# First attention: the sum of squares as two passes over rounded numbers, and the rotation's partner rows projected by extra weight columns

## The reference

```python
kv = (rmsnorm(ckv, ckv_g) @ w_ukv).reshape(B, L, 12, 64 + 64)
k = concatenate([kv[..., :64], broadcast(k_rope, 12 heads, 32)], axis=-1)   # 96 per head
k = rmsnorm(k, k_g)
q = (rmsnorm(h[..., :256], cq_g) @ w_uq).reshape(B, L, 12, 96)
q = rmsnorm(q, q_g)                       # x * rsqrt(mean(x * x) + EPS) * g
# rotation of the last 32 of the 96, on latent tokens:
x1, x2 = x[..., :16], x[..., 16:]
x = concatenate([x1 * cos - x2 * sin, x1 * sin + x2 * cos], axis=-1)
p = softmax(q @ k.T * 96 ** -0.5) ; o = p @ v
```

## Time and profile before

| | |
|---|---|
| median of 3 runs | 3061.49 us (3056.06 to 3071.42) |
| the profiled execution's own time | 3064.81 us, its span 3063.0 us |
| TensorE busy | 2933.3 us, 96% of the span |
| VectorE busy | 1799.2 us, 59% |
| ScalarE busy | 1360.8 us, 44% |
| GpSimd busy | 701.9 us, 23% |

### The profile page before, as it was taken

The page is one execution under the profiler, slowest core; times in us unless marked ns, Lnnn a source line. Parts: engine busy times, 40 slices in busy tenths (PEclk is TensorE's granted clock), DMA queues, the critical chain, the costliest instruction groups (busy, mean ns, idle before and its releaser), DMA issues. The chain is left out here.

```text
span 3063.0 us, 38159 instructions
## 1 busy us (share of the span) xinstructions
PE 2933.3 (96%) x14042; PEld 2109.6 (69%) x14042; DVE 1799.2 (59%) x2476; ACT 1360.8 (44%) x2162; POOL 701.9 (23%) x509
## 2 busy tenths in 40 slices
PE   5998999999999999999999999979999999999999
PEld 2563444444478888889998887844448788888887
DVE  5124656455535877789863444356643887777442
ACT  3014665656633544445653432136662544445231
POOL 0001555455520133330000000034550133331000
PEclk8998999999999999999999999989999999999999
DMA  9920000000020222224664431122211122224453
GB/s 372 369 98 2 4 3 3 4 2 2 7 110 35 77 83 83 83 83 159 210 196 125 145 102 49 41 66 66 64 45 49 63 78 85 84 85 146 137 171 100
DMA packets 101718, 282.14 MB, mean 92 GB/s; under 512 B 12129, under 2 KB 27745, under 8 KB 94562
## 3 DMA queue, kind: packets, MB, share of 16 engines
q1 hardware_dynamic: 101570, 280.16, 27.4%
HBM read 237.25 MB, written 27.26 MB: 86 GB/s over the span
## 5 line engine op out<-in xcount | busy, mean ns | idle before, releaser
L1367 ACT ACTIVATE z_wh<-part 128x512 fp32r<-128x512 f32 x266 | 166.5, 629 | 335.3 <-PE PS L1238 211.4
L1743 DVE TENSOR_TENSOR z_wdl<-part,z_wdh 128x512 fp32r<-128x512 f32 (+3 forms) x208 | 148.7, 721 | 255.5 <-ACT z_wdh L1420 255.2
L1236 PE MATMUL PS<-s_uh,z_wh 128*128 128x512 f32 x736 | 286.6, 389 | 0.0
L1238 PE MATMUL PS<-s_uh,z_wl 128*128 128x512 f32 x736 | 286.6, 389 | 0.0
L1237 PE MATMUL PS<-s_ul,z_wh 128*128 128x512 f32 x736 | 286.5, 389 | 0.0
L1420 ACT ACTIVATE z_wdh<-part 128x512 fp32r<-128x512 f32 (+3 forms) x208 | 135.2, 655 | 303.7 <-DMA part<-in_w_down 302.7
L1664 DVE TENSOR_TENSOR z_wl<-part,z_wh 128x512 fp32r<-128x512 f32 x266 | 218.2, 833 | 46.3 <-ACT z_wh L1367 46.3
L2400 POOL TENSOR_TENSOR X<-X 128x1024 f32<-128x1024 f32 x96 | 229.4, 2389 | 59.6 <-ACT X L2635 58.7
L1223 POOL TENSOR_TENSOR part<-part,part 128x512 f32<-128x512 f32 x38 | 56.8, 1495 | 777.1 <-DMA part<-in_w_up 777.1
L2635 ACT ACTIVATE X<-PS 128x512 f32<-128x512 f32 x252 | 145.9, 593 | 143.8 <-PE PS L2422 135.5
L2731 DVE TENSOR_REDUCE part<-PS 128x1 f32<-128x512 f32 (+1 forms) x312 | 161.9, 580 | 13.7 <-PE PS L2534 12.9
(11 more groups left out here) (412 smaller groups left out, 7594.6 us busy)
## 6 DMA issues: line engine op xcount, KB each, us to landing
part<-in_w_up SPq DMA_DIRECT2D x132, 512.0 KB, 3.3
part<-in_mod_w SPq DMA_DIRECT2D x48, 1024.0 KB, 7.2
part<-in_w_down SPq DMA_DIRECT2D x96, 256.0 KB, 2.7
gated<-part SPq DMA_DIRECT2D x44, 512.0 KB, 2.6
part<-gated SPq DMA_DIRECT2D x87, 256.0 KB, 5.5
part<-in_w_down SPq DMA_DIRECT2D x32, 384.0 KB, 3.1
part<-in_w_down SPq DMA_DIRECT2D x32, 320.0 KB, 3.2
part<-in_w_down SPq DMA_DIRECT2D x48, 192.0 KB, 2.4
```

Source lines behind the costliest of these rows:

```text
L1236: pe.matmul(bank_, w_h, x_h, start=start, stop=False, skip_group_check=further)
L1238: return pe.matmul(bank_, w_l, x_h, start=False, stop=stop, skip_group_check=further)
L1367: act.activation(wh[i][:, :], full[b][i], ACT.Copy).then_inc(s["hi"], 1)
L1743: dve.tensor_tensor(wdl[j][:, :width(e)], wd[j][:, :width(e)], wdh[j][:, :width(e)].bitcast(F32), ALU.subtract).then_inc(s["wdl"], 1)
```

## The change

It does two things in the preparation of each head.

*Sum of squares.* The square is rounded to fp32r by ScalarE (`skh` for keys, `sqh` for queries), VectorE subtracts the rounded number from the square (`square_low`, giving `skl` or `sql`), and `squares` makes two fp32r matmuls by rounded ones (`unity`) into the same bank, in place of one of plain float32. The shared rows 64 to 96 and the ones are rounded once ahead of the loop. `squares` now waits for the subtraction (`sql`) and no longer only for the Square.

*Rotation.* The projection weights of the queries have 128 columns for 96: 32 more hold the partner features in swapped order (`TURNED`). The matmul by `rot0` goes, as does the copy to `raw` of units 3 and 4. VectorE's `turn` has a second operation on 32 rows, partner times gain times signed sine to `raw[64:96]`, and `unit` adds those 32 rows to `t1` and multiplies by the reciprocal root. The sine table has the rows 96 to 128 for this.

```diff
-        WQ = [big(O_A + 8 * T + 20 * 64 + b * 256, 256) for b in range(2)]
+        WQ = [big(O_A + 8 * T + 20 * 64 + b * W_QK, W_QK) for b in range(2)]
...
                         elif w == 5:
                             pe.wait_ge(s["sq"], 6 * p + 5)
-                            pe.wait_ge(s["t1"], 2 * p + 2)
+                            pe.wait_ge(s["ts"], 2 * p + 2)
...
                             for k in range(2):
-                                mm = pe.matmul(ps(PB[w], hi - lo, slice(0, A_QK)), wq[b][:, 96 * k:96 * k + 96],
+                                mm = pe.matmul(ps(PB[w], hi - lo), wq[b][:, k * P:(k + 1) * P],
...
                     def squares(p, w):
-                        pe.wait_ge(s["sq"], 6 * p + w + 1)
-                        if w == 4:
-                            pe.wait_ge(s["out"], 6 * p + 4)
+                        pe.wait_ge(s["sql"], 6 * p + w + 1)
                         at_least(pe, "lo", 6 * p + w - 1)
-                        src = sk[0:A_QK, lo:hi] if w < 3 else sq[w % 2][0:A_QK, :hi - lo]
-                        pe.matmul(ps(NB[w % 2], hi - lo, slice(0, A_QK)), ones[0:A_QK, 0:A_QK], src,
-                                  start=True, stop=True).then_inc(s["nt"], 1)
-                        if 3 <= w < 5:
-                            if w == 3:
-                                pe.wait_ge(s["t1"], 2 * p + 1)
-                            pe.matmul(ps(TB, hi - lo, slice(0, A_QK)), rot0[:, 0, :],
-                                      raw[w % 2][0:A_QK, :hi - lo], start=True, stop=True).then_inc(s["rt"], 1)
+                        for x in (skh, skl) if w < 3 else (sqh[w % 2], sql[w % 2]):
+                            part = x[0:A_QK, lo:hi] if w < 3 else x[0:A_QK, :hi - lo]
+                            mm = pe.matmul(ps(NB[w % 2], hi - lo, slice(0, A_QK)), unity[0:A_QK, :], part,
+                                           start=x in (skh, sqh[w % 2]), stop=x in (skl, sql[w % 2]))
+                        mm.then_inc(s["nt"], 1)
...
                             act.activation(sk[0:64, lo:hi], ps(PB[w], n, slice(0, 64)), ACT.Square).then_inc(s["sq"], 1)
+                            act.wait_ge(s["sq"], 6 * p + w + 1)
+                            act.activation(skh[0:64, lo:hi], sk[0:64, lo:hi], ACT.Copy).then_inc(s["sqh"], 1)
...
                             act.activation(sq[w % 2][0:96, :n], ps(PB[w], n, slice(0, 96)), ACT.Square)\
                                 .then_inc(s["sq"], 1)
+                            act.wait_ge(s["sq"], 6 * p + w + 1)
+                            act.activation(sqh[w % 2][0:96, :n], sq[w % 2][0:96, :n], ACT.Copy).then_inc(s["sqh"], 1)
...
+                    act.activation(skh[64:96, :], sk[64:96, :], ACT.Copy).then_inc(s["kh0"], 1)
+                    act.activation(unity[:, :], ones[:, 0:A_QK], ACT.Copy).then_inc(s["kh0"], 1)
...
-                        dve.wait_ge(s["rt"], v + 1)
-                        T_ = ps(TB, n, slice(0, 96))
-                        dve.tensor_tensor(T_, T_, rope[0:96, 1, lo:hi], ALU.mult).then_inc(s["ts"], 1)
                         dve.wait_ge(s["ts"], v + 1)
-                        dve.tensor_tensor(t_, t_, T_, ALU.add).then_inc(s["ta"], 1)
+                        dve.tensor_tensor(t_[64:96], t_[64:96], raw[w % 2][64:96, :n], ALU.add).then_inc(s["ta"], 1)
...
+                        dve.scalar_tensor_tensor(out=raw[w % 2][64:96, :n], in0=ps(PB[w], n, slice(96, P)),
+                                                 scalar=sml[96:P, W_G0:W_G0 + 1], in1=rope[96:P, 1, lo:hi],
+                                                 op0=ALU.mult, op1=ALU.mult).then_inc(s["ts"], 1)
+
+                    def square_low(p, w):
+                        lo, hi = CH[w % 3]
+                        n = hi - lo
+                        dve.wait_ge(s["sqh"], 6 * p + w + 1)
+                        if w < 3:
+                            out_, in_, h_ = skl[0:64, lo:hi], sk[0:64, lo:hi], skh[0:64, lo:hi]
+                        else:
+                            out_, in_, h_ = [x[w % 2][0:96, :n] for x in (sql, sq, sqh)]
+                        dve.tensor_tensor(out_, in_, h_.bitcast(F32), ALU.subtract).then_inc(s["sql"], 1)
...
                         if kind == "prep" and 3 <= n < 5:
                             turn(p, n)
+                        if kind == "prep" and n < 6:
+                            square_low(p, n)
                         if kind == "prep" and 0 < n < 7:
                             unit(p, b, n - 1)
...
+                    dve.wait_ge(s["kh0"], 1)
+                    dve.tensor_tensor(skl[64:96, :], sk[64:96, :], skh[64:96, :].bitcast(F32), ALU.subtract).then_inc(s["kh0"], 1)
```

More of the change, by code:

```diff
@@ L40 @@
 A_SCALE = A_QK ** -0.5
+TURNED = [*range(A_QK), *range(80, 96), *range(64, 80)]
+W_QK = 2 * P + A_NOPE
 C_HEADS, C_KV, C_HD = 12, 4, 64
@@ L88, in rope @@
         return np.cos(a).T.astype(np.float32), np.sin(a).T.astype(np.float32)
-    rope0 = np.zeros((A_QK, 2, T), np.float32)
+    rope0 = np.zeros((P, 2, T), np.float32)
     rope0[:, 0] = 1
@@ L94, in constants @@
         rope0[b:b + 16, 0, :SEQ], rope0[b:b + 16, 1, :SEQ] = cs, sn
+    rope0[96:112, 1], rope0[112:128, 1] = -rope0[64:80, 1], rope0[80:96, 1]
     rope1 = np.zeros((P, 2, T), np.float32)
@@ L2074, in _ @@
                     sp.wait_ge(s["ab"], 7)
-                    sp.dma_start(ROPE[0:A_QK], a["rope0"]).then_inc(s["tab"], 16)
+                    sp.dma_start(ROPE[:, :, :], a["rope0"]).then_inc(s["tab"], 16)
                 @block.gpsimd
@@ L2267, in heads0 @@
             assert o == O_A + 8 * T + 20 * 64
-            o += 512
+            o += 2 * W_QK
             wq = WQ
@@ L2274, in heads0 @@
             rest += 2 * T
-            raw, sq = [[Xf[:, rest + (2 * x + n) * BANK:rest + (2 * x + n + 1) * BANK] for n in range(2)] for x in range(2)]
-            t1 = [take(BANK) for _ in range(2)]
+            raw, t1 = [[Xf[:, rest + (2 * x + n) * BANK:rest + (2 * x + n + 1) * BANK] for n in range(2)] for x in range(2)]
+            sql = [place(f"h0_sql{n}", o + n * BANK, BANK) for n in range(2)]
+            sq = [take(BANK) for _ in range(2)]
+            sqh = [place(f"h0_sqh{n}", 9088 + n * BANK, BANK) for n in range(2)]
             lnb = take(BANK)
@@ L2280, in heads0 @@
             osb = take(BANK + P)
+            skh, skl = place("h0_skh", O_MIX + 5 * T, T), place("h0_skl", -(-o // 32) * 32, T)
+            unity = place("h0_unity", 10 * A_HEADS * 64, A_QK)
             rope = ROPE
@@ L2302, in heads0 @@
                      ("one", "one1", "pad", "pad1", "S", "P", "PV", "raw", "rawc",
-                      "sq", "nt", "rt", "ln", "rinv", "t1", "ts", "ta", "out", "hi", "lo", "cast", "vs", "mx", "mc", "mn", "mrow",
+                      "sq", "sqh", "sql", "kh0", "nt", "ln", "rinv", "t1", "ts", "ta", "out", "hi", "lo", "cast", "vs", "mx", "mc", "mn", "mrow",
                       "mr", "o", "bc", "lnr", "rs", "fin", "ad")}
@@ L2488, in project @@
                         if w < 3:
-                            mm = pe.matmul(ps(PB[w], hi - lo, slice(0, 64)), wq[b][:, 192:256], H[:, 2, lo:hi],
+                            mm = pe.matmul(ps(PB[w], hi - lo, slice(0, 64)), wq[b][:, 2 * P:W_QK], H[:, 2, lo:hi],
                                            start=True, stop=True)
@@ L2524, in step @@
                             for c, (lo, hi) in enumerate(CH):
-                                if (n, c) == (0, 1):
-                                    pe.wait_ge(s["out"], 6 * p + 5)
                                 if (n, c) == (0, 2):
@@ L2585, in project @@
                             act.activation(sk[0:64, lo:hi], ps(PB[w], n, slice(0, 64)), ACT.Square).then_inc(s["sq"], 1)
+                            act.wait_ge(s["sq"], 6 * p + w + 1)
+                            act.activation(skh[0:64, lo:hi], sk[0:64, lo:hi], ACT.Copy).then_inc(s["sqh"], 1)
                         else:
                             at_least(act, "nt", 6 * p + w - 1)
-                            if w == 3:
-                                at_least(act, "out", 6 * p)
-                            act.activation(raw[w % 2][0:96, :n], ps(PB[w], n, slice(0, 96)), ACT.Copy)\
-                                .then_inc(s["rawc"], 1)
+                            if w == 5:
+                                act.wait_ge(s["ta"], 2 * p + 1)
+                                act.activation(raw[1][0:96, :n], ps(PB[w], n, slice(0, 96)), ACT.Copy)\
+                                    .then_inc(s["rawc"], 1)
                             act.activation(sq[w % 2][0:96, :n], ps(PB[w], n, slice(0, 96)), ACT.Square)\
                                 .then_inc(s["sq"], 1)
+                            act.wait_ge(s["sq"], 6 * p + w + 1)
+                            act.activation(sqh[w % 2][0:96, :n], sq[w % 2][0:96, :n], ACT.Copy).then_inc(s["sqh"], 1)
                     def inverse(p, w):
@@ L3615 @@
     put(W_CKVG, cols(f["mla_ckv_g"][0]))
-    put(W_G0, f["mla_q_g"].T)
```

(3 more changed lines are left out.)

## The result

| | before | changed |
|---|---|---|
| median in one comparison | 3061.96 us | 3102.27 us (3098.90 to 3103.00, 4 runs) |
| ratio | | 1.0128, 95% interval 1.0113 to 1.0144 |
| the profiled execution's own time | 3064.81 us | 3098.90 us, its span 3097.1 us |
| TensorE busy | 2933.3 us | 2903.2 us |
| VectorE busy | 1799.2 us | 1882.0 us |

The change makes the kernel 40 us slower, with TensorE busy 30 us less. The forecast was 34 us more.

What follows compares the result with a forecast made beforehand. The ScalarE and VectorE chain up to VectorE's reduces, not TensorE, was taken to bound the kernel: 11 x 2.55 + 6 = 34 us on 3061.5 gives 3095 us. Likeliest case 3084 to 3107 (0.61); 8 in 10 from 3070 to 3115.

Steps and rivals of the forecast that it cites:

- The chain: Preparation of a head: square, sum, Ln, Exp, normalise, round, remainder on ScalarE and VectorE decides when the reduces start, not TensorE.
- The walk: Step-by-step timing of one head's six units from 397.25 us: reduces at 425.48 for 422.93, 2.55 us more a head.
- TensorE's waits: In a head's preparation: 6.4 us after the change, where before has about 0.4.
- its savings: TensorE work saved: 2.0 us on sums of squares and 1.8 on rotations, 3.8 us a head, 42 us over eleven preparations.
- The width of the projection: Query projection with 32 more outputs: costed at nothing, upper bound 1.4 us.
- The blocked subtractions: Units 2 and 4: a VectorE subtraction with two SBUF inputs waits for GpSimd's add; recorded over 1.5 and over 1 us.
- The rival without blocks: Subtractions each take 0.69 us at once: +0.8 us a head, +15 in all, 3076 us; chance 0.16.
- the case of a longer chain: Adds block a third subtraction or 32-row sum, or waits lower TensorE's clock: + 25 us, 3120 us; chance 0.10.
- The sum: Whole kernel: 11 x 2.55 + 6 = 34 us more, carried to the median: 3095 us.
- The first preparation: Start of the attention, with nothing to hide it: first normalising at 266.1, end at 284.8 for 278.76, +6 us.
- The 11 heads: Preparations in the attention loop: each 2.55 us longer, 11 x 2.55.
- a row of few partitions: VectorE's two new 32-row products: about the 0.7 us that a 512 operation takes whatever its rows.

Runs made afterwards that it cites:

- Experiment 6: Changed kernel with the squares summed in one rounded pass, remainders left out: 3050.2 us against 3061.4 before, ratio 0.9961.
- experiment 4: Only the rotation's half of the change, sum of squares left as one plain float32 matmul: 3055.5 us against 3059.5 before, ratio 0.9979.
- 9: Experiment 6 with four overwritten plain float32 matmuls a head in TensorE's waits: 3048.8 us against 3062.1 before, ratio 0.9953.
- 8: Experiment 4 with three overwritten plain float32 matmuls a head ahead of the maxima: 3045.1 us against 3061.4 before, ratio 0.9946.
- experiment 1: Changed kernel with squares of keys and of units 4 and 5 left in PSUM: 3094.3 us against 3059.5 before, ratio 1.0107.
- 2: Changed kernel with GpSimd's adds in rounds 3 and 4 cut to 32 columns, first add a memset: 3091.7 us against 3059.5 before, ratio 1.0088.
- 5: Changed kernel with unit 1 normalised on VectorE ahead of the subtraction of unit 2: 3097.9 us against 3061.4 before, ratio 1.0120.
- experiment 3: Only the two-pass rounded sum of squares, rotation by the `rot0` matmul as before: 3117.2 us against 3059.5 before, ratio 1.0181.
- experiment 11: Changed kernel, squares in SBUF, with four overwritten matmuls a head in TensorE's waits: 3096.9 us against 3062.1 before, ratio 1.0116.
- 10: Kernel before the change with three overwritten matmuls a head ahead of the maxima, a control: 3063.4 us against 3062.1 before, ratio 1.0003.
- 7: Experiment 1 with four overwritten plain float32 matmuls a head in TensorE's waits: 3080.8 us against 3061.4 before, ratio 1.0070.

## Why the prediction was right, point by point

**The chain sets the time, not TensorE: shown.** The reduces moved by 2.7 us a head (forecast 2.55) while TensorE's busy time in that part fell by 2.7 where no low stretch lies in it. Experiment 6 takes another 2.9 us of TensorE's work away from the part of experiment 4 and leaves it as long, and with the waits filled (9 against 8) the time doesn't fall either. The halves of the change go the same way: rotation alone shortens the chain by 1.2 us, squares alone lengthen it by 4.1 to 5.6, of which some may be the clock's.

**The walk.** Set against the timeline of the head that starts at 409.05 (11.80 later than the walk's start), it has the sum of unit 0 at 414.5 (measured 414.45), the rounding of unit 1 at 421.96 (421.96), that of unit 3 at about 431.0 (431.11) and the reduces at 437.28 (437.47). TensorE's waits were put too long: 6.4 us a head, where the three entries for the new subtraction and the partner product come to 4.6. So were its savings, though nothing hung on them: a pair of rounded sums takes 0.54 us and not 0.46 (0.31 from the first to the second, then 0.23). The width of the projection was costed at nothing, which is right: two passes of 512 columns with 128 outputs take 1.71 us from start to start (509.82 to 511.53 in experiment 4), and with 96 outputs 1.72 (410.19 to 411.91 before).

**The blocked subtractions: shown.** 2.23 and 1.23 us where the walk has 2.2 and 1.5, each held until GpSimd's add is through. They fall to 0.42 and 0.69 when one operand is in PSUM (experiment 1) or when the add is short (2), and that of unit 2 also when VectorE comes to it later (5). The Trainium skill's page SBUF — State Buffer, section "Who interferes with whom", says the same: a VectorE instruction with two SBUF inputs and a GpSimd instruction that reads SBUF block one another in full, the later one waiting, and a tensor_tensor with only one input in SBUF doesn't contend. These runs agree on both counts: 2.2 against 0.42 us.

**The rival without blocks: its price was wrong.** It was put at 3076, by the walk alone. Experiments 1 and 2 are that case, and measure 3094 and 3092; only with the waits filled is it 3081. What was missing is the low clock in the second part of a head, where it is paid for. The prediction named a falling clock only within the case of a longer chain. It came in the second part where the chain was shorter than the changed kernel's (experiments 1, 2, 4, 5 and 6), in one of ten heads of the changed kernel, and in none of experiment 3, whose chain is longer still. In the changed kernel three of the heads of 51.3 have a low stretch in the first part, where TensorE waits anyway, and the other six have none: all nine are equally long, and experiment 11, with fills, has reduces and heads of the same length. So the forecast came out right without a word on the clock. In that it had luck: nothing in it said that the clock would cost the changed kernel 1.6 us in one head of ten, and the kernel of experiment 1 as much in every head.

**The sum: sizes off.** It was 34; the trace has 39.3. The first preparation cost 7.5, not 6. Its first normalising comes 13.04 us behind the start, where before has 6.96: 6.1 more, and the walk has 5.2. From there to the reduces it is 1.4 more, and the walk has 0.9:

```profile
264.53 0.69 DVE L2687 TENSOR_TENSOR PS<-X,PS 96x512 f32<-96x512 f32 x1 [2.00 <-ACT PS L2608]
...
283.77 12.96 DVE L2749 TENSOR_REDUCE part<-PS 128x1 f32<-128x512 f32 x26
```

That part is read from these rows alone; no experiment took it apart. The 11 heads, put at 28.05, took 31.05: 0.1 us a head too little in the walk, and 1.6 us in one piece for the head of 52.93. The last 0.7 (29.69 us from the last Exp but one to the last, before 28.95) was not in the sum. That stretch takes 28.58 to 28.59 us at 0.98 to 1.00 in the traces of experiments 1, 9, 10 and 11, and 29.68 at 0.93 in 4 and 7, so it follows the granted clock, whatever the kernel.

## What to carry to other kernels

- Making an engine faster that is 96% busy gained nothing here, where others decide the hand-over behind its work. Look at what the first waiting instruction behind the preparation waits for; here it was VectorE's reduces, and 40 us came out of a change that saved TensorE 30.
- When splitting a number into a rounded part and its remainder, leave one operand of the subtraction in PSUM if GpSimd is adding at the time (0.42 us in place of 2.2 in experiment 1).
- When a chain has been made shorter and the time stays the same, read the granted clock in the part behind the wait. Three or four matmuls a head whose result is overwritten were worth 10 and 13 us in experiments 8 and 7, 1 us in 9, and nothing in the kernel before. They can be tried on any version in a few lines.

## What the runs showed of the hardware that was not expected

A wait of 1.2 to 1.5 us of TensorE, in the loop of heads, was followed in many heads by a stretch at or near half the full clock (granted 0.50, the 1.2 GHz level, in 428.43 to 431.85 after the change, 0.56 in 436.60 to 440.00 in experiment 1). It costs about 1.6 us where TensorE's work is on the path: 24.51 against 22.89 us for the same part of experiment 4. Not each such wait does it: in the changed kernel the wait of 1.48 us ahead of 438.20 is followed by a part at 1.00, and the low stretch lies ahead of it, at 428.4; and in experiment 4 the heads of 47.4 and of 49.0 are the same program. What decides between them stays open. With the waits filled none of the ten heads of experiments 7, 8, 9 and 11 had such a stretch.

One thing was assumed in the prediction, and is now measured: a row of few partitions was no cheaper on VectorE. The product on 32 x 512 takes 0.76 us (row 427.61), and the one on 96 x 512 takes 0.75.
